# A three-block transformer on one core: row factors of the norms applied after the matmuls

## The reference, cut to what matters

```
first:  x += gate * mixer(modulate(rms_norm(x, g), shift, scale))   # w_in 3072 columns, w_out
        x += gate * moe(modulate(rms_norm(x, g_ffn), ...))           # 16 experts, 1024 x 2816 x 3 weights each
        x  = rms_norm(x, g_final)
second: h  = rmsnorm(x, g_mix) * (1 + scale1) + shift1
        q, k, v, u, vs, ga, gb = split(h @ w_in)                     # 4608 columns (in2)
        x += gate1 * ((sigmoid(ga) * attn(q,k,v) @ wa + sigmoid(gb) * gating(gelu(u), gelu(vs)) @ wb) @ w_out)   # out2
        h  = rmsnorm(x, g_ffn) * (1 + scale2) + shift2
        x += gate2 * (square(relu(h @ w_ff1)) @ w_ff2)               # ff1: 4096 columns, ff2
        x  = rmsnorm(x, g_final)
third, two layers:
        h  = rms_norm(x, pre_norm_g) * (1 + scale) + shift
        q, k, v, g_att, u, b, c, g_conv = split(h @ w_in)            # 4096 columns (in3)
        x += gate * rms_norm(concat(attention, convolution) @ w_out, post_norm_g)      # out3
```

## Time and profile before

| | us |
|---|---|
| median of 3 runs | 2498.31 (2498.10 to 2503.52) |
| the profiled execution's own time | 2495.8 |
| its span | 2493.6 |
| TensorE matmuls busy | 1923.4 (77%) |
| VectorE busy | 714.1 (29%) |
| ScalarE busy | 545.7 (22%) |
| weights read | 756.13 MB, 304 GB/s over the span |
| expert loop, most of its DMA at | 425 GB/s, to about 1693 |
| in2, attention, projections | 1724 to 1890 |
| out2 | 1894 to 1918 |
| ff1, ff2 | 1927 to 2115 |
| in3 with attention, out3, first layer | 2136 to 2294 |
| in3, out3, second layer, last norm | 2318 to 2489 |

### The profile page before, as it was taken

The page is one execution under the profiler, slowest core; times in us unless marked ns, Lnnn a source line. Parts: engine busy times, 40 slices in busy tenths (PEclk is TensorE's granted clock), DMA queues, the critical chain, the costliest instruction groups (busy, mean ns, idle before and its releaser), DMA issues. The chain is left out here.

```text
span 2493.6 us, 34470 instructions
## 1 busy us (share of the span) xinstructions
PE 1923.4 (77%) x14760; PEld 1161.4 (47%) x14760; DVE 714.1 (29%) x1042; ACT 545.7 (22%) x879; POOL 54.1 (2%) x70
## 2 busy tenths in 40 slices
PE   5999887667666766667666666676998999897896
PEld 3786752221121112211112112214887999786785
DVE  4216630000000000000000000006546765556555
ACT  3331221000000000000000000004554654553552
POOL 0005000000000000000000000000000000000000
PEclk8999886655566566665666566658999999898898
DMA  8747479999999999999999999994534455433330
GB/s 343 270 184 271 163 306 395 425 426 426 425 426 425 426 425 426 425 425 426 425 425 426 425 425 425 425 427 148 184 112 144 155 193 174 156 120 101 119 121 33
DMA packets 157965, 760.53 MB, mean 305 GB/s; under 512 B 9751, under 2 KB 101655, under 8 KB 104120
## 3 DMA queue, kind: packets, MB, share of 16 engines
q1 hardware_dynamic: 154216, 754.07, 75.7%
q10 hardware_dynamic: 3664, 5.24, 0.6%
HBM read 756.13 MB, written 3.14 MB: 304 GB/s over the span
## 5 line engine op out<-in xcount | busy, mean ns | idle before, releaser
L793 PE MATMUL ps<-ring,arena 128*32 128x352 f32 x4096 | 624.1, 756 | 237.2 <-DMA ring<-in_w_exp_gate 130.2
L559 PE MATMUL ps<-x_parts,w_hi 128*128 128x256 f32 x2688 | 533.8, 295 | 44.1 <-DVE x_parts L1281 38.0
L559 PEld LDWEIGHTS ps<-x_parts,w_hi 128*128 128x128 f32 x2688 | 441.9, 197 | 73.0 <-issue 45.5
L793 PEld LDWEIGHTS ps<-ring,arena 128*32 128x32 f32 x4096 | 147.4, 153 | 700.6 <-DMA ring<-in_w_exp_up 257.9
L559 PE MATMUL ps<-x_parts,ring_lo 128*128 128x256 f32 x1344 | 389.3, 290 | 0.0
L806 PE MATMUL ps<-ring,arena 128*32 128x256 f32 x2816 | 239.8, 496 | 175.9 <-DMA ring<-in_w_exp_down 129.4
L1247 DVE TENSOR_TENSOR ring_lo<-ring,w_hi 128x1024 fp32r<-128x1024 f32 x220 | 267.5, 1225 | 249.1 <-ACT w_hi L957 241.9
L559 PEld LDWEIGHTS ps<-x_parts,ring_lo 128*128 128x128 f32 x1344 | 266.2, 198 | 0.5 <-issue 0.5
L806 PEld LDWEIGHTS ps<-ring,arena 128*32 128x32 f32 x2816 | 99.7, 136 | 324.6 <-DMA ring<-in_w_exp_down 184.1
L1503 DVE TENSOR_TENSOR arena<-arena,ps 128x704 f32<-128x704 f32 x16 | 14.2, 888 | 824.0 <-PE ps L793 824.0
L957 ACT ACTIVATE w_hi<-ring 128x1024 fp32r<-128x1024 f32 x220 | 229.5, 1051 | 80.1 <-PE ps L914 41.4
(11 more groups left out here) (200 smaller groups left out, 1411.6 us busy)
## 6 DMA issues: line engine op xcount, KB each, us to landing
ring<-in_w_exp_gate SPq DMA_DIRECT2D x128, 1408.0 KB, 10.7
ring<-in_w_exp_up SPq DMA_DIRECT2D x128, 1408.0 KB, 10.9
ring<-in_w_exp_down SPq DMA_DIRECT2D x112, 1536.0 KB, 11.6
ring<-in_w_ada SPq DMA_DIRECT2D x48, 1536.0 KB, 8.7
ring<-in_w_in SPq DMA_DIRECT2D x30, 1536.0 KB, 7.2
ring<-in_w_ff SPq DMA_DIRECT2D x18, 1536.0 KB, 6.9
ring<-in_w_in SPq DMA_DIRECT2D x16, 1024.0 KB, 5.5
ring<-in_w_out SPq DMA_DIRECT2D x8, 1536.0 KB, 7.0
```

The lines of the kernel that those rows point to most:

```text
L559: m = pe.matmul(ps[:, bank, 0:T], w, a, start=(k == 0 and j == 0), stop=(k == KD - 1 and j == 2))
L793: m = pe.matmul(ps[32 * j:32 * j + 32, 2 * (k // 8) + i, 0:FJ // 2], XCUR[:, k % 8, :], ring[:, s, at:at + FJ // 2], start=(k % 8 == 0), s ...
```

## The change

Inputs of in2, ff1 and in3 are now X times a column factor alone (norm gain times 1 + scale), split into `U_HI` and `U_LO`; the row factor is left out. The shift becomes two more input columns (`UCOL` = 258), the second one times 0.125 for the queries. When a block is done, VectorE multiplies it by the row factor from PSUM into one of three `TMP` buffers (`scale_rows`); ScalarE evacuates from there, with the column of the shift as bias (`evacuate_scaled`). The sum of squares is made beside the first unit's matmuls (`column_sums`), from squares by ScalarE added up on VectorE. Where two norms followed one another, the second's mean is worked out from a weighted sum of the same squares (`SUM2`) and both are one step; X itself gets the first norm later, between blocks (`first_norm`). The first unit of every dense layer runs with the chunks outside and its blocks inside (`k_outer`), in in1, out1, out2 and out3 too, and waits for the parts of all its blocks. Turned blocks are gone in in2 and in3: v and vs are made like the others and transposed (`flip`), eight times four transposes. Out2 and ff2 are added to X by VectorE straight from PSUM (`update`), the last expert's too. The post norm of out3 keeps its place, with the columns' factor in the evacuation and squares taken from PSUM. X is stored in four parts. `raised_shift` and `raised_scale` make the columns (operations of 8 to 16 elements), `first_norm` is a reciprocal and eight products.

```diff
+QKV = 10
+FLIP_AT = 12
+FIRST_HEAD = 6
+UCOL = T + 2
...
-    in2 = plan.dense(4608, lambda n: ["lat"], [(8, 12), (16, 20)])
+    in2 = plan.dense(4608, lambda n: ["lat"], flips=[(FLIP_AT, "v"), (21, "vs")])
...
+        R = rs[:, 0:UCOL]
+        R_FIRST = rs[:, 512:512 + T]
+        SUM2 = rs[:, 768:768 + T]
+        S_IN2, S_FF1, S_IN3, GF2_IN2, GF2_IN3, MIX_COL = 0, 1, 2, 4, 5, 6
...
+            for c in range(0, KD, 2):
+                sp.wait_ge(S("x_final"), c + 2)
+                sp.dma_start(out[:, c:c + 2, :], X[:, c:c + 2, :]).then_inc(S("stored"), 16)
+            sp.wait_ge(S("stored"), 16 * KD // 2)
...
+            def k_outer(g, lo, src, first, ready, each):
+                for it in g["items"]:
+                    pe.wait_ge(S("w_split"), it["s"] + 1)
+                    if it["b"] >= 4:
+                        pe.wait_ge(S("evacuated"), it["b"] - 3)
+                for k in range(KD):
+                    pe.wait_ge(S(ready), first + k + 1)
+                    for i, it in enumerate(g["items"]):
+                        x = [a[:, k, :] for a in src(it)]
+                        wl = lo[:, k, it["col"]:it["col"] + P]
+                        for j, (w, a) in enumerate(parts(w_hi[:, it["s"] % HI, k, :], wl, *x)):
+                            m = pe.matmul(ps[:, it["b"] % 4, 0:a.shape[-1]], w, a, start=(k == 0 and j == 0),
+                                          stop=(k == KD - 1 and j == 2), skip_group_check=True)
+                        if k == KD - 1:
+                            count(m, "unit_used" if it["last"] else "block_done")
+                        each(k, i)
+            def flip(it, ready):
+                if it["b"] >= 4:
+                    pe.wait_ge(S("evacuated"), max(it["b"] - 3, ready))
+                for f in range(4):
+                    m = pe.transpose(ps[:, it["b"] % 4, P * f:P * f + P], VF[:, f, P * it["t"]:P * it["t"] + P], ident)
+                count(m, "block_done")
...
+                    if gi == 0:
+                        k_outer(g, lo, src, first, ready, each)
+                        first = None
+                        for it in g["items"]:
+                            if it["last"]:
+                                after(gi)
+                            yield
+                        continue
                     for it in g["items"]:
+                        if "flip" in it:
+                            flip(it, out_by(units, {"v": 11, "vs": 19}[it["flip"]]))
+                            yield
+                            continue
...
+            def column_sums(two, rows=True):
+                if rows:
+                    sums[0] += KD - 1
+                    pe.wait_ge(S("sum1"), sums[0])
+                    m = pe.matmul(ps[:, 5, 0:T], ones, SQ[:, 0, :], start=True, stop=True)
+                if two:
+                    sums[1] += KD
+                    pe.wait_ge(S("sum2"), sums[1])
+                    m = pe.matmul(ps[:, 5, T:2 * T], ones, SUM2, start=True, stop=True)
+                norms[0] += 1
+                count(m, "summed")
+            def raised_dense(units, two):
+                def each(k, i):
+                    if units is in2 and i == 2 and 4 <= k < KD - 1:
+                        for c in range(4) if k == 4 else [k - 1]:
+                            add_column(c)
+                    if k == KD - 1 and i == 0:
+                        if units is in2:
+                            for c in range(KD - 2, KD):
+                                add_column(c)
+                        column_sums(two, units is not in2)
+                return dense_blocks(units, lambda it: (U_HI, U_LO), raise_input(), ready="u_split", each=each)
...
+            def evacuate_scaled(it, dst, func=ACT.Identity, scale=1.0):
+                raised[0] += 1
+                high_parts(it["s"] + HI, group[0])
+                act.wait_ge(S("row_scaled"), raised[0])
+                at = T if scale == 1.0 else T + 1
+                mark(act.activation(dst, TMP[:, it["b"] % 3, 0:T], func, scale=scale,
+                                    bias=TMP[:, it["b"] % 3, at:at + 1]), "evacuated")
+            def raise_x(s_col, c, name, value):
+                act.wait_ge(S(name), value)
+                mark(act.activation(U_HI[:, c, 0:T], X[:, c, :], ACT.Copy, scale=col(s_col, c)), "u_high")
+                mark(act.activation(SQ[:, c, :], X[:, c, :], ACT.Square), "x_squared")
+            def roots(two):
+                root_no[0] += 1
+                act.wait_ge(S("mean_square"), root_no[0])
+                mark(act.activation(rs[:, 0:T], rs[:, 0:T], ACT.Sqrt), "rooted")
+                if two:
+                    mark(act.activation(R_FIRST, R_FIRST, ACT.Sqrt), "rooted_first")
...
+            for c in range(KD):
+                raise_x(S_IN2, c, "x_new", c + 1)
+            roots(True)
...
             for g in out2:
                 for it in g["items"]:
-                    evacuate(it, SQ[:, it["n"], :], ACT.Copy, mod[:, 2, 16 + it["n"]:17 + it["n"]])
-            modulate(H, mod[:, 3, 0:8], high=X_HI)
+                    high_parts(it["s"] + HI)
+                    raise_x(S_FF1, it["n"], "evacuated", it["b"] + 1)
+            roots(False)
             for g in ff1:
                 for it in g["items"]:
-                    evacuate(it, HFF[:, it["n"], :], ACT.Relu)
+                    evacuate_scaled(it, HFF[:, it["n"], :], ACT.Relu)
...
+            def add_square(c, gain2=None, rows=True):
+                x_squares[0] += 1
+                waits("x_squared", x_squares[0])
+                if gain2 is not None and c == 0:
+                    mark(ts(SUM2, SQ[:, 0, :], col(gain2, 0), None, ALU.mult), "sum2")
+                elif gain2 is not None:
+                    waits("sum2", made["sum2"])
+                    mark(stt(SUM2, SQ[:, c, :], col(gain2, c), SUM2, ALU.mult, ALU.add), "sum2")
+                if rows and c > 0:
+                    if c > 1:
+                        waits("sum1", made["sum1"])
+                    mark(tt(SQ[:, 0, :], SQ[:, 0, :], SQ[:, c, :], ALU.add), "sum1")
+            raised = [0]
+            def raise_low(s_col, c):
+                raised[0] += 1
+                waits("u_high", raised[0])
+                mark(stt(U_LO[:, c, 0:T], X[:, c, :], col(s_col, c), U_HI[:, c, 0:T].bitcast(F32),
+                         ALU.mult, ALU.subtract), "u_split")
...
+            def row_roots(two):
+                norms[0] += 1
+                waits("summed", norms[0])
+                if two:
+                    link(ts(R_FIRST, ps[:, 5, 0:T], 1.0 / D, EPS, ALU.mult, ALU.add))
+                    link(stt(rs[:, 0:T], R_FIRST, EPS, ps[:, 5, T:2 * T], ALU.mult, ALU.add), "mean_square")
+                else:
+                    link(ts(rs[:, 0:T], ps[:, 5, 0:T], 1.0 / D, EPS, ALU.mult, ALU.add), "mean_square")
+                waits("rooted", norms[0])
+                link(dve.reciprocal(rs[:, 0:T], rs[:, 0:T]))
+            scaled_rows = [0]
+            def scale_rows(it):
+                waits(*it["done"])
+                if it["b"] >= 3:
+                    waits("evacuated", it["b"] - 2)
+                mark(tt(TMP[:, it["b"] % 3, :], ps[:, it["b"] % 4, 0:UCOL], R, ALU.mult), "row_scaled")
...
             low_parts(starts["in2"] + 3)
-            rms(X, V("g_final", 0, 8), by="scaled", then=final_square)
-            rms(X, V("g_mix_2", 0, 8), mod[:, 2, 8:16], then=low_modulated)
-
+            waits("scattered", EXPERTS + 1)
+            for i in range(KD + 2):
+                if i < KD:
+                    mark(stt(X[:, i, :], ps[:, 4 + i // 2, T * (i % 2):T * (i % 2) + T], mod[:, 1, 16 + i:17 + i],
+                             X[:, i, :], ALU.mult, ALU.add), "x_new")
+                if 1 <= i <= KD:
+                    raise_low(S_IN2, i - 1)
+                if i >= 2:
+                    add_square(i - 2, GF2_IN2, rows=False)
+            row_roots(True)
...
+                        i, it = next(items)
+                        if "flip" not in it:
+                            low_parts(it["s"] + HI)
+                            scale_rows(it)
+                        if gain is not None:
+                            first_norm(i, gain)
...
+            def update(it, gate):
+                waits(*it["done"])
+                dve.scalar_tensor_tensor(X[:, it["n"], :], ps[:, it["b"] % 4, 0:T], gate[:, it["n"]:it["n"] + 1],
+                                         X[:, it["n"], :], ALU.mult, ALU.add).then_inc(S("evacuated"), 1)
+            waits("x_normed", KD)
+            for g in out2:
+                for it in g["items"]:
+                    update(it, mod[:, 2, 16:24])
+                    low_parts(it["s"] + HI)
+                    raise_low(S_FF1, it["n"])
+                    add_square(it["n"])
+            row_roots(False)
+            def square_out(it):
+                n = it["n"]
+                waits("ff_high", n + 1)
```

(68 more changed lines are left out.)

193 lines of the change are left out of this document (128 added, 65 removed).

## The result

The changed kernel takes 2526.05 us (2521.12 to 2529.51, four runs), the kernel before 2498.2 (2494.71 to 2503.52, four runs beside it): a ratio of 1.0108 with a 95% interval of 1.0082 to 1.0134. It is 1.1% slower. The forecast was 2497 with a range of 2456 to 2524, so the time lies 2 us beyond the range's upper end and 29 us above the forecast.

What follows compares the result with a forecast made beforehand. The expert loop waits for weights; dense layers are bound by TensorE, with serial norms between. Terms summed to -1.7 against the profiled 2495.8: 2494.1, or 2497 for the median, range 2456 to 2524.

Steps and rivals of the forecast that it cites:

- the ring: Per block, high part, low part, row scaling and evacuation run in series: 3.16 us, 3.60 in ff1, where TensorE needs 2.86.
- ff1 and ff2: From out2's end to ff2's end: 212.7 us where it was 197.0, +15.7 (+8 to +22).
- The first rival: TensorE's slack of four weight blocks hides the ring, each block 2.86 us; median 2426; 12%.
- the serial parts: out2 +3.3, out3 -5 each, in3's first `max_of` at 44.5 us, in2's first `max_of` -12.8, end -3.
- The gap behind the k-outer unit: At a layer's start, TensorE has done its three blocks and idles some 4 us.
- the attention phases: Heads in in2 and in3, priced within terms of +3.5 for in2, -5.2 and 0 for in3's two layers.
- last rival: in2 and in3 lose by left-out waits what other stages gain; upper end of the forecast's range; no chance of its own.
- the pitches of heads: in2's attention: head 0 takes 18.1 us, heads with four, three and two blocks 15.6, 12.5 and 9.2.
- The clock rival: TensorE busy 79% in ff1 lowers the clock, blocks at 5.1 us; half of ff1's blocks so, +24: 2521; 14%.
- The table switch rival: A table switch costs twice its row: 7 heads x (1.3 + 0.9) = +15, 2512; 4%.
- in1 and out1: Ahead of the experts, k-outer fills the wait for input columns: -6 us (0 to -8).

Runs made afterwards that it cites:

- the doubled step: Every `scale_rows` done twice: in the changed kernel 2581.8 us; in the changed kernel with `pair_out` early and `scale_rows` ahead of the low parts 2422.82 us.
- the exchanged order: The changed kernel with `scale_rows` put ahead of `low_parts` on VectorE: 2454.97 us, ratio 0.9823.
- pair early: The changed kernel with `pair_out` right behind the next even head's division: 2483.55 us, 0.9942 against before.
- pair early in it: The kernel before with `pair_out` right behind the next even head's division: 2478.45 us, ratio 0.9918.
- the kernel with both edits: The changed kernel with `pair_out` behind the next even head's division and `scale_rows` ahead of `low_parts`: 2415.64 us, ratio 0.9686.
- the fourth block ahead: The kernel with both edits, plus the fourth weight block's high and low parts ahead of the norm's roots in in2, ff1 and in3: 2414.25 us.

## Why the prediction was wrong, point by point

- **Right: the ring and its price.** 3.09 and 3.54 us a block against 3.16 and 3.60; ff1 and ff2 +15.1 against +15.7. The first rival (the ring doesn't pace) fell in the first trace, and the doubled step and the exchanged order show the mechanism.
- **Right: the serial parts.** out2, out3, and in3's start (44.1 against 44.5 us from ff2's end to the first `max_of`) within half a microsecond, in2's start and the end 4 and 3 us better than forecast. The gap behind the k-outer unit is 5.08 us in in2, 3.37 in ff1, 3.83 and 3.37 in in3, where I wrote some 4.
- **Wrong: the attention phases, the step that failed.** In the terms for in2 and in3 I summed rings, `max_of`, exp and the copy of the probabilities for each head, and left the wait of `values` for `pair_out` out. The prediction names it only in its last rival ("waits between `scores`, `values` and `max_of` that I left out"), gives it no price of its own, and puts it at the upper end of the forecast's own range, 2515. Measured, the three terms are +12.6, +7.9 and +10.8 instead of +3.5, -5.2 and 0: 33 us, more than the whole error of 27 between the spans. With this wait taken away (pair early) the pitches of heads come out as I priced them: heads with four, three and two blocks (and no flips) at 15.0 to 15.3, 11.9 to 12.5 and 8.8 us against 15.6, 12.5 and 9.2; head 0 17.3 to 17.9 against 18.1. Its span of 2482.2 lies 10 us below the forecast's 2491.9: the other terms together were that much too slow, and by luck hid a part of what the missing wait cost.
- **The row that I should have asked.** The group of `values` (L860) in the trace of before shows 18.2 us of idleness, 13.5 of them until VectorE's L1636, which is `pair_out` in in3. A wait that is already in the profile, for an instruction at the end of a VectorE queue, can grow with whatever the change puts into that queue: these 13.5 us became 26.0.
- **The clock rival** is refuted, though its time (2521) is nearer to the measured one than the forecast. The granted clock in ff1 is 1.00 with TensorE busy 90%. I had expected 79%; with a step doubled it is 78% there (70.33 of 90 us), and the clock is still 0.96. The clock did cost something at another place, in the `values` and `scores` behind the even heads' waits: over the whole kernel these two groups are busy 33.6 and 29.4 us in the changed kernel, 25.9 and 23.8 with pair early, 13 us less.
- **The table switch rival**: in the changed kernel the 14 table loads ahead of evacuations (L1083) take 18.0 us, 1.28 each, as in the earlier trace rows. In the kernel with pair early an evacuation ends at 2207.95, a load starts at 2207.97, and the exp behind it at 2209.26, 0.01 us after the load's end. The drain that the Trainium skill states, "ScalarE: Activation LUTs", section "What ACT_TABLE_LOAD costs", does not show here either.
- **in1 and out1** measured -9.7 in one pair of profiled executions. The nine traces with the changed kernel's instructions up to that point ended the expert loop at 1684.8 to 1696.5, 1689.3 in the mean; the two with those of before (before, and pair early in it) at 1694.5 and 1696.5. So a single pair gives anything between +2 and -12, and the mean, some 5 to 7 us less, fits the forecast of -6 without settling it.

## What to carry to other kernels

Where two engines each issue "prepare block s+3, then finish block s" and the finishing now goes from one to the other, write down the ring and count how many blocks it spans: one block means that its steps add up, and to swap two lines (finish first, then prepare) makes it two. And before pricing a change, list every consumer that waits for the last instruction in the queue that you make longer; here one copy out of PSUM, at the end of a head, held up the other engine's next head.

## What was not expected of the hardware

Executions whose instructions are the same up to the experts differ there by some 10 us, and the clock that was granted differs with it. TensorE is busy 36.0 of the 40 us from 200 to 240 us in both of these; the windows, first the kernel with both edits, then that with the fourth block ahead as well (it differs only behind the experts):

```profile
200.00:240.00 40.00, 36.03 (x324) 25.82 (x316) 22.41 (x27) 2.92 (x4) 17.45 (x18) 0.91 0.74 276
```

```profile
200.00:240.00 40.00, 36.02 (x277) 26.18 (x275) 19.65 (x23) 2.43 (x3) 17.99 (x18) 0.80 0.70 261
```

The first does 324 matmuls at a clock of 0.91, the second 277 at 0.80, and their first expert matmuls start at 383.3 and 393.1 us. The expert stage carries that on to its end (1685.2 and 1696.5). All nine traces with these instructions go the same way: at 0.91 (four) the expert loop ended at 1684.8 to 1685.2, at 0.82 or 0.83 (three) at 1690.0 to 1691.0, at 0.80 (two) at 1696.2 and 1696.5. What decides between the two was not tried; it is why a term of a few microseconds in this stretch can't be read from one pair of traces.
